# A Trainium2 block kernel: raw token transposes, the norm kept as a row, adaLN units in pairs, gate matmuls over half the rows, and two loads asked for later

## The reference, cut to what matters

```python
mod_l = split(silu(c) @ w_ada + b_ada, 6); mod_c = split(silu(c_ctx) @ w_ada + b_ada, 6)
n_lat = modulate(rmsnorm(x, g_norm1), mod_l[0], mod_l[1])     # t * (1 + scale) + shift
n_ctx = modulate(rmsnorm(ctx, g_norm1), mod_c[0], mod_c[1])
z = n @ w_in                      # columns u (S5), v (RG-LRU), g, gate a, gate b
ya = glu(s5(u)); yb = rglru(conv(v)) * gelu(g)
#   rglru: r = sigmoid(x_heads @ w_r + b_r), i = sigmoid(x_heads @ w_i + b_i), 16 heads of 64
#   a = exp(-8 r softplus(-lambda)); h = scan(a, sqrt(1 - a^2) * i * x), both directions
m = sigmoid(ga) * (ya @ w_proj_a) + sigmoid(gb) * (yb @ w_proj_b)
h = x + mod_l[2] * (m @ w_out)
f = modulate(rmsnorm(h, g_norm2), mod_l[3], mod_l[4])
h = h + mod_l[5] * peer_ffn(f)    # 8 heads, top 16 of 16384 experts, rows of peer_u and peer_v gathered
out = rmsnorm(h, g_final)
```

## Time and profile before

| | |
|---|---|
| time, median of 3 runs | 2401.45 us (2401.24 to 2403.92) |
| the profiled execution's own time | 2391.49 us |
| its span, first to last instruction | 2389.7 us |
| PE busy | 2042.9 us (85%) |
| DVE busy | 1382.9 us (58%) |
| POOL busy | 1040.6 us (44%) |
| ACT busy | 434.7 us (18%) |
| data moved by DMA | 789.32 MB, mean 330 GB/s |

### The profile page before, as it was taken

One profiled execution on the slowest core, in us unless ns is written; L12 is line 12 of the kernel. 1 busy time (PEld: TensorE's weight loads), 2 busy tenths in 40 slices (PEclk: granted clock), 3 DMA queues, 4 the chain that ended last, 5 costly groups with the idle time before them and its releaser, 6 DMA issues.

```text
span 2389.7 us, 21847 instructions
## 1 busy us (share of the span) xinstructions
PE 2042.9 (85%) x8162; PEld 1186.7 (50%) x8162; DVE 1382.9 (58%) x2112; ACT 434.7 (18%) x937; POOL 1040.6 (44%) x884
## 2 busy tenths in 40 slices
PE   5999999999999999989789889777777777777776
PEld 4444447888888878875344445222222222222222
DVE  2634552699996443546545664665566566655644
ACT  4014540233332000011011111101110111111011
POOL 1001005599994010034454454555555555555552
PEclk9999999999999999999999999999999999999999
DMA  9964448555666897869999999999999999999996
GB/s 314 306 211 128 169 177 191 177 184 180 193 191 205 306 377 289 295 251 410 413 414 418 420 421 421 422 421 421 422 422 421 421 422 421 421 422 421 422 422 249
DMA packets 253016, 789.32 MB, mean 330 GB/s; under 512 B 25160, under 2 KB 170768, under 8 KB 177520
## 3 DMA queue, kind: packets, MB, share of 16 engines
q0 software_dynamic: 80528, 558.18, 57.6%
q1 hardware_dynamic: 160704, 220.31, 27.7%
q10 hardware_dynamic: 11680, 9.44, 1.3%
HBM read 774.20 MB, written 9.47 MB: 328 GB/s over the span
## 4 chain that ended last, share of the span: by engine, by line
DMA 38%; PE 22%; issue 1%; POOL 1%; DVE 0%; ACT 0%; DVEq 0%; ACTq 0%; POOLq 0%
DMA vb<-in_peer_v,eidx 38%; PE ps L1970 12%; PE ps L1871 4%; PE ps L1926 4%; PE ps L1903 1%; POOL vb L1567 0%; DMA w_ring<-in_w_out 0%; PE ps L1890 0%; PE ps L1941 0%; POOL nT L1567 0%; DVE h L1809 0%; POOL mT L1567 0%; DVE f L1808 0%; DVE h L1816 0%; ACT L1642 0%
## 5 line engine op out<-in xcount | busy, mean ns | idle before, releaser
L1970 PE MATMUL ps<-vb,diag 128*128 128x512 f32 x2048 | 954.8, 613 | 274.4 <-DMA vb<-in_peer_v,eidx 270.1
L1970 PEld LDWEIGHTS ps<-vb,diag 128*128 128x128 f32 x2048 | 378.6, 193 | 840.8 <-DMA vb<-in_peer_v,eidx 439.1
L1567 POOL DMA_INDIRECT vb<-in_peer_v,eidx x256 | 420.0, 1640 | 552.7 <-PE ps L1970 542.7
L1835 DVE CUSTOM_DVE_ANT_0 nT<-nT,f 128x2048 f32<-128x2048 f32 x170 | 389.3, 2292 | 341.6 <-DMA nT<-in_peer_u,eidx 341.2
L1237 PE MATMUL ps<-nT,w_ring 128*128 128x256 f32 (+1 forms) x1600 | 425.4, 424 | 0.8 <-issue 0.8
L1237 PEld LDWEIGHTS ps<-nT,w_ring 128*128 128x128 f32 x1600 | 302.8, 191 | 112.7 <-issue 80.6
L1835 DVE CUSTOM_DVE_ANT_0 mT<-mT,f 128x2048 f32<-128x2048 f32 x86 | 197.1, 2292 | 186.5 <-DMA mT<-in_peer_u,eidx 186.4
L1673 ACT ACTIVATE gel<-hd 128x2 f32<-128x2 f32 x128 | 26.0, 204 | 1119.0 <-DVE hd L1835 1119.0
L1567 POOL DMA_INDIRECT nT<-in_peer_u,eidx x170 | 171.7, 1010 | 51.8 <-issue 51.8
L1871 PE MATMUL ps<-w_ring,mT 128*128 128x256 f32 x512 | 111.7, 380 | 5.2 <-PEq L258 2.9
L1567 POOL DMA_INDIRECT mT<-in_peer_u,eidx x86 | 89.0, 1035 | 47.4 <-issue 25.9
(11 more groups left out here) (364 smaller groups left out, 2099.2 us busy)
## 6 DMA issues: line engine op xcount, KB each, us to landing
w_ring<-in_w_ada SPq DMA_DIRECT2D x96, 1024.0 KB, 5.7
w_ring<-in_w_in SPq DMA_DIRECT2D x50, 1024.0 KB, 5.3
w_ring<-in_w_out SPq DMA_DIRECT2D x16, 1024.0 KB, 7.6
w_ring<-in_peer_w_query SPq DMA_DIRECT2D x16, 1024.0 KB, 25.1
w_ring<-in_w_proj_b SPq DMA_DIRECT2D x8, 1024.0 KB, 9.0
w_ring<-in_w_proj_a SPq DMA_DIRECT2D x8, 1024.0 KB, 7.9
big<-in_w_in ACTq DMA_DIRECT2D x6, 768.0 KB, 4.9
big<-big SPq DMA_DIRECT2D x128, 32.0 KB, 3.6
```

What stands on the lines that cost most here:

```text
L1567: pool.indirect_dma_start(ring[m % n], None, table, bass.IndirectOffsetOnAxis(ap=eidx[:, i % 3, j:j + 1], axis=0))\
L1835: v.tensor_tensor_reduce(ub[m % n_u], ub[m % n_u], f[:, i // HEADS], 1.0, 0.0, ALU.mult, ALU.add, hd[:, i % 2, m % K:m % K + 1]).then_inc( ...
L1970: last = pe.matmul(ps[:, 4 * tile + c, :], diag[:, m % NDIAG], vb[m % NV][:, c * 512:(c + 1) * 512], start=(r == 0), stop=(r == HEADS * K ...
```

## The change

Six edits in one:

1. **Raw transposes.** The token blocks are transposed as they are, by the identity, as soon as the tokens are there: 16 PSUM tiles of four transposes, first the context's eight, then the latent's. DVE copies them to `nT`, not ACT.
2. **The norm as a row.** A matrix of ones times the four diagonals gives 1/rms of the 512 tokens as a row on all partitions (`rstd_row`). In each group DVE multiplies by scale and by this row in one instruction, for both k and both halves, and ACT adds the shift (four instructions).
3. **Pairs of units.** The units of the next group are multiplied two behind product 1 and two behind product 5, and the columns come behind product 9.
4. **Loads asked for later.** `w6[0]` is issued when the raw transposes are copied, `w6[1]` behind the first `group_rows`, and the S5 output weights `cnat` when three units of group 0 are used. They are transposed in groups 1 and 2, two blocks at a time behind products 0, 2, 4, 6, and ACT copies them.
5. **Setup arithmetic** on exponents and angles stands behind group 0's scaling on DVE and ACT (`angles`), ahead of `w6[2]` and `w6[3]` on ACT.
6. **Gates as row halves.** `bd` holds no zeros: the even head's r and i weights lie side by side on partitions 0 to 63, the odd head's (i, r) on 64 to 127. A gate matmul contracts 64 rows, the two halves write different banks, and ACT takes eight sigmoids of 64 partitions instead of four of 128. The zeroing of `mT` goes.

```diff
@@ pool
+            pool.wait_ge(ada_used, 3)
             for r, name in enumerate(("s5_c_re", "s5_c_im")):
...
             pool.wait_ge(w6_used, 2)
-            pool.memset(mT[:], 0.0).then_inc(bd_zero, 1)
-            pool.wait_ge(bd_zero, 1)
             pool.wait_ge(ada_used, NFIRST * KD - 2)
...
+                        pool.dma_start(bd[e * 64:(e + 1) * 64, :, d, (x + e) % 2, :], src[e]).then_inc(bd_in, 16)
@@ scalar
-            load_w6(0)
-            load_w6(1)
...
-            for i in (2, 0, 3, 1):
+            for i in range(4):
...
-            for k in range(KD):
-                act.wait_ge(nt_tr, k + 1)
-                act.activation(nT[:, k, :], ps[:, 2 + k % 4, :], ACT.Copy).then_inc(nt_raw, 1)
+            act.wait_ge(nt_raw, KD)
+            load_w6(0)
+
+            def output_weights(n):
+                r, j = divmod(n, 4)
+                act.wait_ge(tr_s5, n + 2)
+                act.activation(Cc[:, r, j * 16:(j + 1) * 16, :].rearrange("p g h -> p (g h)"), ps[:, 1, 256:512],
+                               ACT.Copy, scale=-1.0 if r else 1.0).then_inc(s5_setup, 1)
...
             group_rows(0)
+            load_w6(1)
             for g in range(NG8):
-                act.wait_ge(norm_ready, g + 1)
-                for k in (2 * g, 2 * g + 1):
-                    act.activation(nT[:, k, 0:T], nT[:, k, 0:T], ACT.Identity, scale=mcol[:, 0, k, 1:2],
-                                   bias=mcol[:, 1, k, 1:2]).then_inc(nt_ctx, 1)
+                for n in range(4):
+                    k, x = 2 * g + n // 2, n % 2
+                    act.wait_ge(nt_scaled, 4 * g + n + 1)
+                    act.activation(nT[:, k, x * T:(x + 1) * T], nT[:, k, x * T:(x + 1) * T], ACT.Identity,
+                                   bias=mcol[:, 1, k, 1 - x:2 - x]).then_inc(nt_done, 1)
+                if g == 0:
+                    act.activation(sm[:, 1, :], sm[:, 0, :], ACT.Exp).then_inc(dt_done, 1)
...
+                    act.activation(sm[:, 9, :], sm[:, 7, :], ACT.Sin, scale=0.5).then_inc(sin_done, 1)
+                    load_w6(2)
+                    load_w6(3)
...
+                if g in (1, 2):
+                    for n in range(4 * g - 4, 4 * g - 1):
+                        output_weights(n)
                 if g + 1 < NG8:
                     group_rows(g + 1)
+                if g in (1, 2):
+                    output_weights(4 * g - 1)
@@ scalar, gates
-                for n in range(4):
-                    d, x = n // 2, n % 2
-                    act.wait_ge(g_full, 4 * k + n + 1)
-                    act.activation((rt, ig)[x][:, b, d, :], ps[:, 2 + n, :], ACT.Sigmoid,
...
+                for d in range(2):
+                    act.wait_ge(g_full, 2 * (2 * k + d + 1))
+                    for x, dst in enumerate((rt, ig)):
+                        for e in range(2):
+                            to, at = slice(e * 64, (e + 1) * 64), (x + e) % 2
+                            act.activation(dst[to, b, d, :], ps[at * 64:(at + 1) * 64, 2 + 2 * d + e, :], ACT.Sigmoid,
@@ vector
+            for n in range(KD):
+                x, kk = divmod(n, KD // 2)
+                v.wait_ge(nt_tr, n + 1)
+                v.tensor_copy(nT[:, 2 * kk:2 * kk + 2, x * T:(x + 1) * T],
+                              ps[:, 4 + n % 4, :].rearrange("p (e c) -> p e c", e=2)).then_inc(nt_raw, 1)
+                if n == KD - 3:
+                    v.wait_ge(ss_done, 4)
...
+            v.wait_ge(rstd_full, 1)
+            v.tensor_copy(rstd_row, ps[:, 1, :]).then_inc(rstd_ready, 1)
...
-                    tsc(nT[:, k, T:2 * T], nT[:, k, T:2 * T], mcol[:, 0, k, 0:1], mcol[:, 1, k, 0:1],
-                        ALU.mult, ALU.add).then_inc(nt_lat, 1)
+                    for x in range(2):
+                        nk = nT[:, k, x * T:(x + 1) * T]
+                        stt(nk, nk, mcol[:, 0, k, 1 - x:2 - x], rstd_row[:, x * T:(x + 1) * T], ALU.mult, ALU.mult)\
+                            .then_inc(nt_scaled, 1)
+                if g == 0:
+                    angles()
@@ tensor
+            for x in range(2):
+                for i in range(2):
+                    pe.wait_ge(x_in[2 * x + i], 16)
+                for kk in range(KD // 2):
...
+                    for j in range(4):
+                        k = 2 * kk + j // 2
+                        last = pe.transpose(ps[:, 4 + n % 4, j * P:(j + 1) * P], xt[2 * x + j % 2][:, k * P:(k + 1) * P],
+                                            ident[:])
...
+            for i in range(4):
+                last = pe.matmul(ps[:, 1, i * P:(i + 1) * P], ones, diagx[:, i], start=True, stop=True)
...
+            for x in range(4):
+                group_unit(0, x)
             group_columns(0)
             for g in range(NG8):
                 for m in range(2 * NB):
                     front_product(g, m)
+                    if g in (1, 2) and m in (0, 2, 4, 6):
+                        output_weights(4 * g - 4 + m // 2)
                     if g + 1 < NG8:
-                        if m in (0, 2, 4, 7):
-                            group_unit(g + 1, (0, 2, 4, 7).index(m))
-                        if m == 10:
+                        if m in (1, 5):
+                            group_unit(g + 1, m // 2)
+                            group_unit(g + 1, m // 2 + 1)
+                        if m == 9:
...
-                for i in range(4):
-                    pe.matmul(ps[:, 2 + i, :], (bd, bd2)[i // 2][:, k, i % 2, :], xc[:, k % 4], start=True, stop=True)\
-                        .then_inc(g_full, 1)
+                for d in range(2):
+                    for e in range(2):
+                        half = slice(e * 64, (e + 1) * 64)
+                        pe.matmul(ps[:, 2 + 2 * d + e, :], bd[half, k, d].rearrange("p x c -> p (x c)"),
+                                  xc[half, k % 4], start=True, stop=True).then_inc(g_full, 1)
```

More of the change, by code:

```diff
@@ L1207, in group_columns @@
                     pe.wait_ge(sel_ready, 1)
+                    pe.wait_ge(rstd_ready, 1)
                 else:
@@ L1255, in lag_zero @@
                         last.then_inc(kz_full, 1)
+            for x in range(2):
+                for i in range(2):
+                    pe.wait_ge(x_in[2 * x + i], 16)
+                for kk in range(KD // 2):
+                    n = x * KD // 2 + kk
+                    if n >= 4:
+                        pe.wait_ge(nt_raw, n - 3)
+                    for j in range(4):
+                        k = 2 * kk + j // 2
+                        last = pe.transpose(ps[:, 4 + n % 4, j * P:(j + 1) * P], xt[2 * x + j % 2][:, k * P:(k + 1) * P],
+                                            ident[:])
+                    last.then_inc(nt_tr, 1)
             pe.wait_ge(mrow_in, 16 * 2)
@@ L1260, in _ @@
             pe.transpose(ps[:, 2, 32:120], prow[:], ident[0:88, 0:88]).then_inc(tr_setup, 1)
-            pe.wait_ge(s5_in, 16 * 9)
+            pe.wait_ge(ones_ready, 1)
+            pe.wait_ge(diagx_done, 4)
+            for i in range(4):
+                last = pe.matmul(ps[:, 1, i * P:(i + 1) * P], ones, diagx[:, i], start=True, stop=True)
+            last.then_inc(rstd_full, 1)
+            pe.wait_ge(s5_in, 16 * 5)
             for r in range(2):
@@ L1264, in _, with output_weights @@
             pe.transpose(ps[0:H, 3, 2 * G:3 * G], dnat, ident[0:G, 0:G]).then_inc(tr_s5, 1)
-            for r in range(2):
-                for k in range(KW):
-                    last = pe.transpose(ps[:, 4 + 2 * r + k // 4, (k % 4) * P:(k % 4 + 1) * P], cnat[:, r, k], ident[:])
-            last.then_inc(tr_s5, 1)
-            pe.wait_ge(diagx_done, 4)
-            pe.wait_ge(setup_read, 1)
-            pe.wait_ge(s5_setup, 4)
-            for k in range(KD):
-                if k >= 4:
-                    pe.wait_ge(nt_raw, k - 3)
-                for i in range(4):
-                    last = pe.matmul(ps[:, 2 + k % 4, i * P:(i + 1) * P], xt[i][:, k * P:(k + 1) * P], diagx[:, i],
-                                     start=True, stop=True)
-                last.then_inc(nt_tr, 1)
-                if k in (7, 8, 11, 12):
-                    group_unit(0, (7, 8, 11, 12).index(k))
+            pe.wait_ge(nt_raw, KD)
+            def output_weights(n):
+                if n == 0:
+                    pe.wait_ge(s5_in, 16 * 9)
+                else:
+                    pe.wait_ge(s5_setup, n)
+                r, j = divmod(n, 4)
+                for k in range(2):
+                    last = pe.transpose(ps[:, 1, (2 + k) * P:(3 + k) * P], cnat[:, r, 2 * j + k], ident[:])
+                last.then_inc(tr_s5, 1)
+            for x in range(4):
+                group_unit(0, x)
             group_columns(0)
-            pe.wait_ge(nt_raw, KD)
             for g in range(NG8):
@@ L1294, in gates @@
                 if k >= 1:
-                    pe.wait_ge(g_sig, 4 * k)
+                    pe.wait_ge(g_sig, 8 * k)
                 else:
```

97 lines of the change are left out of this document (45 added, 52 removed).

## The result

| | median us | ratio to before, 95% interval |
|---|---|---|
| before, 4 runs | 2402.68 (2401.24 to 2404.51) | |
| changed kernel, 4 runs | 2380.62 (2378.94 to 2381.40) | 0.9912 [0.9887, 0.9937] |
| changed kernel again, 6 runs beside 11 of before | 2381.58 beside 2402.81 | 0.9917 [0.9897, 0.9937] |

The change makes the kernel 20 us faster (by the second ratio 15 to 25). The forecast was 2380. That number came out, but the sum under it did not: the stages that the change touches gave 14 us, not 21.3. The rest of this document is about those two differences.

A forecast was written before the change was run, and what follows sets the result against it. The front (to 184 us) and the column stage with gates decide; later work, ended by the `peer_v` gathers, shifts along. Front 12.6 + gates 8.7 = 21.3 us off 2401.45 gives 2380, range 2372 to 2392.

The forecast's parts named there:

- unit four: Front, group 0: fourth `w_ring` load lands at 27.4 us, or 29.6 with `w6[0]` in front, instead of 35.7.
- Unit eight: Front: last ring load group 0 needs lands at 51.0 us, between 47.7 (`w6[2]` to `w6[4]` behind) and 54.3 (ahead).
- The rule that was cited beside it: DMA engines take turns between queues by packet, so `w6`'s 3 KB rows go ahead of 1 KB ring rows; sum 3.3 us worse.
- From the unit to group 1: Front: unit matmuls 1.0 us, products 6 to 9 3.6, slow clock 1.6, columns 0.8, chain 2.6; group 1 starts at 60.6.
- Period: Front, groups 1 to 7: 3.0 us less over six periods, cancelled by 3.2 us of output-weight transposes.
- Output weights: Front: eight pairs of `cnat` transposes cost PE 3.2 us in all, with ACT idle enough not to add more.
- the wait at `lag_zero`: End of column stage: ACT and DVE chain 2.4 us longer, PE 1.5 shorter, margin 0.4, so PE waits 3.5 us.
- The term of 8.7 us: Column stage: eight gate slots save 12.2 us, less 3.5 us of PE waiting at the end, leaving 8.7.
- nothing in the middle waits: Column stage: ACT, busy about 10 us per column, has 15.6 or more, so its extra sigmoids delay nothing before the end.
- halves in line: Gates: the two 64-row halves do not overlap, gaining nothing; time 2391 us. Part of a 16% rival.
- ACT setting the pace in every column: Gates: ACT's eight sigmoids limit every column and give back the 12.2 us; time 2389. Part of a 16% rival.
- Late output weights: Front, group 1: PE waits for S5 loads if `cnat` lands after 82 us; at 90 us, time 2410. Chance 3%.

The follow-up runs named there:

- the front alone: The changed kernel with the gates as before (four matmuls over 128 rows, zeroed block-diagonal weights, four sigmoids): 2385.21 us, ratio 0.9942.

## Why the prediction was right in its number, and where its sum was wrong

- **Raw transposes and the norm as a row** did what was said: unit four landed at 27.4, the earlier of the two values worked out (the sum went on from the later, 29.6), and group 0's first product came at 36.3 (35 forecast). What is late next is the units: right.
- **Unit eight** was put at 51.0, the middle between 47.7 and 54.3; it landed at 55.1. This is the first term that was mis-sized, by 4.1 us. Taking the middle was a choice without a row. The rule that was cited beside it gave 54.3, and the packets bear it out. The DMA terms themselves were right: from its issue unit eight took 23.6 us in the changed kernel, 17.0 with the three `w6` behind it (6.6 less, 6.6 forecast) and 12.7 without `cnat` as well (4.3 less, 3.9 forecast). Wrong was how much of the 6.6 stands ahead: all, not half.
- **From the unit to group 1**: 9.6 forecast, 10.0 measured, slow clock included.
- **Period**: six periods took 97.7 us, 2.2 less than before (99.9), where nothing was forecast. Output weights cost 0.9 a group, not 1.6: 16.9 in groups 1 and 2 against 16.0. With this the front gave 10.4 to 11.0, not 12.6.
- **Gates**: the slot was right (1.9), and so was the wait at `lag_zero` (3.5 forecast, 3.0 and 3.2 measured). That wait came out right as two errors cancelled: eight sigmoids took 5.63 us, not 4.84, and PE came to `lag_zero` some 1.0 later than worked out, held by a late unit. The term of 8.7 us failed all the same; it measured 3.1 to 3.5 in the changed kernel and nothing on the kernel before. The step that failed is "nothing in the middle waits": I asked only whether ACT can follow. The late `w_ada` units need their time to land too, and they had it with almost nothing to spare. Four waits of 3.3 us in all take it back, 3.8 with what stands around them (a pair of units with a wait took 2.6 to 3.0 us, one without 1.85, the last pair before 2.2). Another 0.1 us goes at each half column beside a change of tile shape (7.06 where it was 6.96), 1.6 in all. With the 3.2 at `lag_zero` that is 8.6 of 12.1 us.
- **The rest**: touched stages give 14.0 to 14.1 us in like pairs of traces, timed runs 19.9 [15, 25]. The missing 6 would have to lie behind `lag_zero`, where the three traces with the old front took 2024 to 2035 us and eight with the new one 2021 to 2029. That is what the spread of executions does as well: the spans of two like pairs differ by 12.6 us (2389.7, 2377.1) and by 26.0 (2400.8, 2374.8). Whether the untouched stages gain a few microseconds from their phase against DMA stays open. That the forecast of 2380 met the median to within 1 us is luck: the sum was 7 us too large in the touched stages, and 6 came from where it had none.
- **Rivals**: halves in line, and ACT setting the pace in every column, are both out. So the Trainium skill's warning on emptying PSUM (TensorEngine Tiling (Array Packing), PSUM Bottleneck) holds here only at the last gates, through DVE's chain, where it costs 3 us (no wait there with the front alone, whose gates are the old ones). Late output weights never held PE: `cnat` landed by 46.4.

## What to carry to other kernels

Ask of every engine's time that is taken away what it was covering: not only the engine that must follow, but each load whose landing was timed by it. Loads on a second queue are not behind the first queue's loads because they were asked for later; count packets, and ask for them one at a time where a ring is being waited for. When a first trace and the timed runs differ by more than the effect, profile the old kernel again before the difference is explained.

## What the runs showed of the hardware that was not expected

- Two queues with work took exact turns by packet (498 and 498, 884 and 884 in 5 us), so a queue with rows three times as long got 1.43 MB of 1.94.
- A 64-partition sigmoid of 512 elements took 682 ns, that of 128 partitions 688.
- Two matmuls over 64 rows each, into different banks with 128 output columns, ran side by side: four in 1.92 us where four over 128 rows took 3.43.
- A run of 256 very small matmuls held a gap of 2 to 6 us for which the profile names no cause. DMA was full in the short and in the long ones. A packet of the `instruction` queue stood at each, two at the longest (5.4 and 6.1); that PE waited for its instructions is not shown.
